# A gated embedding at the end of a mixture-of-experts phase: its projection computed ahead of it for all eight row tiles, and a wait moved in an attention loop

## What is computed

```python
# attention, per block of 128 query rows and per head (4 heads, values 128 wide)
prob = jax.nn.softmax(jnp.where(causal, sc, neg), axis=-1)
attn = prob[:, :, 0] - lam * prob[:, :, 1]
blocks.append(jnp.einsum('bhqk,bhkv->bhqv', attn.astype(v.dtype), v[:, :, :end]))

# after the mixture of experts: x is (1024, 1024), p is (1024, 256)
x = x + hierarchical_moe(rms_norm(x, norm_ffn[l]), ...)
ple_gate = jax.nn.sigmoid(rms_norm(x, norm_ple[l]) @ w_ple_gate[l])   # (1024, 1024)
x = x + ple_gate * (p[l] @ w_ple_proj[l])                             # (256, 1024)
```

## Time and profile before

| | us |
|---|---|
| median of 3 runs | 3212.57 (3206.74 to 3223.68) |
| the profiled execution | 3211.77 |
| its span, first to last instruction | 3209.9 |

### The profile page before, as it was taken

One profiled execution on the slowest core, in us unless ns is written; L12 is line 12 of the kernel. 1 busy time (PEld: TensorE's weight loads), 2 busy tenths in 40 slices (PEclk: granted clock), 3 DMA queues, 4 the chain that ended last, 5 costly groups with the idle time before them and its releaser, 6 DMA issues. The chain is left out here.

```text
span 3209.9 us, 52447 instructions
## 1 busy us (share of the span) xinstructions
PE 2899.2 (90%) x21080; PEld 2499.3 (78%) x21080; DVE 1898.4 (59%) x2347; ACT 1276.7 (40%) x1825; POOL 752.8 (23%) x474
## 2 busy tenths in 40 slices
PE   7999999888786897699999969799999998878898
PEld 7999997777454786588888848699999975756687
DVE  4365666775464543889898955420068668686411
ACT  3000015564554322588877743221111167443311
POOL 3222213332000000222221101168332252222300
PEclk9999999998687998799999979899999998896999
DMA  5457341001103732799999963534757662222411
GB/s 177 160 193 245 121 143 48 33 33 60 40 14 116 257 118 112 281 401 398 403 401 393 396 236 117 141 102 156 240 190 231 203 220 89 95 98 64 137 69 49
DMA packets 195579, 560.14 MB, mean 175 GB/s; under 512 B 26208, under 2 KB 99936, under 8 KB 169200
## 3 DMA queue, kind: packets, MB, share of 16 engines
q1 hardware_dynamic: 150000, 461.97, 40.0%
q10 hardware_dynamic: 34624, 64.17, 5.4%
q0 software_dynamic: 10752, 31.13, 3.1%
HBM read 440.10 MB, written 124.30 MB: 176 GB/s over the span
## 5 line engine op out<-in xcount | busy, mean ns | idle before, releaser
L437 PE MATMUL pin_psum<-pin_sb_w,pin_sb_hT 128*128 128x354 f32 (+1 forms) x5376 | 981.2, 344 | 15.2 <-DVE pin_sb_hT L373 6.0
L437 PEld LDWEIGHTS pin_psum<-pin_sb_w,pin_sb_hT 128*128 128x128 f32 x5376 | 938.0, 190 | 54.7 <-issue 8.1
L4510 DVE TENSOR_TENSOR moe_sb_wlo<-moe_sb_raw,moe_sb_whi 128x2048 fp32r<-128x2048 f32 x192 | 433.8, 2286 | 69.5 <-ACT moe_sb_whi L4279 69.5
L4279 ACT ACTIVATE moe_sb_whi<-moe_sb_raw 128x2048 fp32r<-128x2048 f32 x192 | 365.4, 1917 | 103.9 <-PE moe_psum L4649 77.6
L345 ACT ACTIVATE pin_sb_xt<-pin_psum,pin_sb_ss 128x353 f32<-128x353 f32 (+1 forms) x112 | 63.4, 587 | 508.8 <-PE pin_psum L437 433.3
L408 DVE TENSOR_SCALAR pin_sb_xt<-pin_psum,pin_sb_ss 128x353 f32<-128x353 f32 (+1 forms) x112 | 69.0, 625 | 294.3 <-PE pin_psum L437 294.1
L4649 PE MATMUL moe_psum<-moe_sb_whi,moe_sb_xhi 128*128 128x512 f32 x512 | 204.2, 399 | 8.4 <-DVE moe_sb_xlo L4514 8.4
L4649 PE MATMUL moe_psum<-moe_sb_whi,moe_sb_xlo 128*128 128x512 f32 x512 | 201.0, 393 | 0.0
L4649 PE MATMUL moe_psum<-moe_sb_wlo,moe_sb_xhi 128*128 128x512 f32 x512 | 200.5, 392 | 0.0
L294 POOL TENSOR_TENSOR pin_sb_w<-pin_sb_raw,pin_sb_w 128x2832 fp32r<-128x2832 f32 (+1 forms) x26 | 186.9, 7188 | 22.5 <-issue 19.8
L292 POOL CAST pin_sb_w<-pin_sb_raw 128x2832 fp32r<-128x2832 f32 (+1 forms) x26 | 74.4, 2863 | 486.1 <-PE pin_psum L437 462.7
(11 more groups left out here) (714 smaller groups left out, 5668.2 us busy)
## 6 DMA issues: line engine op xcount, KB each, us to landing
moe_sb_raw<-in_w_gate SPq DMA_DIRECT2D x64, 1024.0 KB
moe_sb_raw<-in_w_up SPq DMA_DIRECT2D x64, 1024.0 KB, 7.8
moe_sb_raw<-in_w_down SPq DMA_DIRECT2D x64, 1024.0 KB, 7.6
scratch_proj<-pin_sb_xt ACTq DMA_DIRECT2D x16, 1412.0 KB, 8.7
scratch_proj<-pin_sb_xt ACTq DMA_DIRECT2D x12, 1792.0 KB, 7.3
pin_sb_raw<-in_w_in SPq DMA_DIRECT2D x15, 1412.0 KB, 9.6
pin_sb_raw<-in_w_in SPq DMA_DIRECT2D x11, 1792.0 KB, 8.9
scratch_ybuf<-moe_sb_yb ACTq DMA_DIRECT2D x32, 512.0 KB, 8.3
```

Source lines behind the costliest of these rows:

```text
L437: mm = te.matmul(ps[:, t, 0:cols], hT[a_part][:, k, t * P:(t + 1) * P], wt[b][w_part][:, k, :], start=(k == 0 and n == 0), stop=(k == KD - ...
L4279: s.activation(whi[q][:, :, :], raw[q][:, :, :], ACT.Copy).then_inc(hi, 1)
L4510: tt(wlo[q][:, :, :], raw[q][:, :, :], whi[q][:, :, :].bitcast(F32), ALU.subtract).then_inc(lo, 1)
```

## The change

In **attention**, `output` no longer waits for both rounds of `flat_out` before its first instruction. The two transposes have no such wait, the first four matmuls wait for the first round alone, and the others for the second.

In **`moe_ple`**:

- p comes in one transfer of 1 MB (`pt`, all tiles) ahead of the weights, instead of 128 KB per tile beside `xt`.
- The weight tiles are loaded and split in another order: the two of the projection first.
- PE turns p of four tiles at a time (`turn_p`, eight transposes), once before the last `down` and once after it; ACT and DVE split each four (`round_p`, `rest_p`).
- PE computes all eight projections (`product_p`) right after the last `down`, into three pairs of banks in turn, in the order of tiles 1 to 7 and then 0. ACT copies the first six into SBUF (`keep_p`), four of them into the buffers `l_raw` once these are free; the last two stay in PSUM.
- `turn`, `copy` and `body` of the loop lose what they did with p: two transposes, one rounding, one subtraction, 12 matmuls per tile. `finish` reads the kept projection from SBUF (PSUM for tiles 7 and 0) and multiplies in place.
- One root of a dummy value, before the first `norm`, brings ACT's table for the root in ahead of time.

```diff
@@ class Attention, output
-                te.wait_ge(flat_out, rounds_to(i + 1))
                 te.wait_ge(kept, i + 1)
                 if t + 1 < NT:
                     for a in pair:
                         te.transpose(ps[:, 7, (2 + a) * P:(3 + a) * P], qk[t + 1][...], ident[:, :])
                 for k in range(t + 1):
+                    if k % 4 == 0:
+                        te.wait_ge(flat_out, rounds_to(i) + k // 4 + 1)
                     mm = te.matmul(ps[:, 7, 0:AV], aT[i % 2][:, k * P:(k + 1) * P], vv[k][...], start=(k == 0), stop=(k == t))
@@ moe_ple
+    W_ORDER = (KD, KD + 1, *range(KD))
+    P_ORDER, P_BANKS, KEPT = (*range(1, NT), 0), (2, 4, 6, 2, 4, 6, 2, 6), NT - 2
...
@@ sync
                 sp.dma_start(xt[b][:, :], x[t * P:(t + 1) * P, :]).then_inc(l_x_in[b], 16)
-                sp.dma_start(pt[b][:, :, :].rearrange("p a c -> p (a c)"), p[t * P:(t + 1) * P, :]).then_inc(l_x_in[b], 16)
...
+            sp.wait_ge(xt_ps, last_n + 1)
+            sp.dma_start(pt[:, :, :], p.rearrange("(t p) c -> p t c", p=P)).then_inc(p_in, 16)
             sp.wait_ge(lo, item(last_n, 1))
@@ scalar
-                s.activation(hThi[b][:, :, :], hT[:, :, :], ACT.Copy)
-                s.activation(pThi[b][:, :, :], blocks(ps, 2, 2), ACT.Copy).then_inc(rounded.sem, 1)
+                s.activation(hThi[b][:, :, :], hT[:, :, :], ACT.Copy).then_inc(rounded.sem, 1)
...
+            def round_p(i):
+                s.wait_ge(p_turned, i + 1)
+                s.activation(p_hi[i][:, :, :], blocks(ps, 0, 8), ACT.Copy).then_inc(p_high, 1)
+            def keep_p(j):
+                s.wait_ge(p_sums, j + 1)
+                if j >= 2:
+                    s.wait_ge(w_lo, KW)
+                s.activation(p_kept[j][:, :], banks(ps, P_BANKS[j]), ACT.Copy).then_inc(p_out, 1)
...
+            s.activation(ss[1][:, 2:3], ss[1][:, 2:3], ACT.Sqrt)
@@ vector
-                tt(pTlo[b][:, :, :], blocks(ps, 2, 2), pThi[b][:, :, :].bitcast(F32), ALU.subtract).then_inc(copied.sem, 1)
...
-                tt(m[:, :], l_sg[:, :], banks(ps, 6), ALU.mult)
+                tt(l_sg[:, :], l_sg[:, :], part, ALU.mult)
                 ve.drain()
-                tt(x_t[:, :], x_t[:, :], m[:, :], ALU.add).then_inc(added.sem, 1)
+                tt(x_t[:, :], x_t[:, :], l_sg[:, :], ALU.add).then_inc(added.sem, 1)
@@ tensor
+            def turn_p(i):
+                if i == 0:
+                    te.wait_ge(p_in, 16)
+                else:
+                    te.wait_ge(p_low, i)
+                for n in range(8):
+                    mm = te.transpose(block_of(ps, 0, n), pt[:, P_ORDER[4 * i + n // 2], ...], ident)
+                mm.then_inc(p_turned, 1)
+            def product_p(j):
+                i, at = j // 4, 2 * (j % 4)
+                if j % 4 == 0:
+                    te.wait_ge(p_low, i + 1)
+                if j == 0:
+                    te.wait_ge(w_lo, 2)
+                if j == 1:
+                    te.wait_ge(y_ev, last_n + 3)
+                if j >= 3:
+                    te.wait_ge(p_out, P_BANKS[:j][::-1].index(P_BANKS[j]) * -1 + j)
+                ...   # 12 matmuls into banks P_BANKS[j] and the next one
+            turn_p(0)
             down(last_n, tail=True)
+            turn_p(1)
+            for j in range(NT):
+                product_p(j)
@@ body(t)
-                te.wait_ge(added.sem, added.done(t - 1))
-                for half in range(2):
-                    for k in range(2):
-                        mm = product(6, proj_rows, b, KD, 2, half, k)
-                mm.then_inc(proj_sums.sem, 1)
```

More of the change, by code:

```diff
@@ L4124, in moe_ple @@
                       for i, n in enumerate(("hThi", "hTlo")))
-        xt = [put(f"xt{b}", [P, D], home["xb"] + D * b) for b in range(2)] + [put(f"xt{b}", [P, D], home["yb"] + D * (b - 2)) for b in (2, 3)]
-        pt = [put(f"pt{b}", [P, 2, P], home["xT"] + 2 * P * b) for b in range(AHEAD)]
-        pThi, pTlo = ([put(f"{n}{b}", [P, 2, P], home["xT"] + D + 2 * P * (2 * i + b), F32R) for b in range(2)]
-                      for i, n in enumerate(("pThi", "pTlo")))
+        xt = [put(f"xt{b}", [P, D], home["xT"] + D * b) for b in range(2)] + [put(f"xt{b}", [P, D], home["yb"] + D * (b - 2)) for b in (2, 3)]
+        pt = put("pt", [P, NT, 2 * P], home["xb"])
+        p_hi, p_lo = [put("p_hi0", [P, KD, P], home["a"], F32R), hThi[1]], [put("p_lo0", [P, KD, P], late, F32R), hTlo[1]]
+        p_kept = [put("p_kept0", [P, D], home["a"] + D), put("p_kept1", [P, D], late + 2 * D), *l_raw]
         l_sg = put("l_sg", [P, D], home["a"])
@@ L4708, in product @@
                 return mm
-            gate_rows, proj_rows = (hThi, hTlo), (pThi, pTlo)
+            gate_rows = (hThi, hTlo)
             def gate_half(t, half):
```

98 lines of the change are left out of this document (62 added, 36 removed).

## The result

| | kernel before | changed kernel |
|---|---|---|
| median | 3211.73 (3206.74 to 3223.68, 4 runs) | 3173.78 (3171.04 to 3175.19, 4 runs) |
| profiled execution, its span | 3211.77, 3209.9 | 3174.87, 3173.0 |

The ratio is 0.9874, 95% interval 0.9856 to 0.9893. The forecast was 3187, its range 3178 to 3201: the direction was right, the time 13 us too high and outside the range.

A forecast was written before the change was run, and what follows sets the result against it. The prediction saw PE's stops on a ring with ACT bounding wide attention, and PE, closely followed by a DVE-ACT ring, the embedding's loop. 8.4 + 3.1 + 0.6 + 10.1 + 2.2 = 24.4 us off 3211.77 gave 3187, range 3178 to 3201.

The forecast's parts named there:

- 8.7 + 0.7 - 1.0 = 8.4: Attention: us gained from PE's stops in wide steps, less what stays in tile 7; bounds 3 to 9.4.
- a swinging clock: Rival in the embedding's loop: PE's new pauses make its clock swing mildly, about 1.2 us a tile, 3194; chance 0.12.
- Cover of 0.75 against stops of 0.54: Attention: two transposes and four matmuls, 0.75 us, cover PE's wait for the second copy, 0.54 on average, 0.8 at most.
- The expected rest in tile 7: Attention: tile 7 lacks transposes, 0.5 us of cover against 0.7; some 0.25 may stay in each of four steps.
- Between experts and embedding: PE's added projections and ACT's copies fit the 24.80 us idle gap before the loop: cost 0, upper bound some 20 us.
- ACT ends near 1911: Between experts and embedding: ACT's copies and dummy root end near 1911, against idle until 1911.63; tight, but covered.
- First tile: Embedding's first tile: table load 1.1 us earlier, stretch from `turn(0)` 6.7 to 4.7; together -3.1, bounds -1.5 to -4.6.
- The loop: Embedding's loop, body(1) to the last sigmoid: six tiles from 89.3 to 79.2 us, -10.1, bounds -6 to -13.
- The ring: Embedding's loop: DVE and ACT, weigh to weigh, 14.03 falling to 13.1 us; x's load makes it 13.4 in four tiles.
- both slow-clock rivals: Embedding's loop: PE's clock swings mildly, 3194, chance 0.12; or the half behind each pause runs at 1.2 GHz, 3218, 0.04.
- The tail: Embedding's end: `finish` of the last tile no longer waits for the projection, -2.2 us.
- p's transfer: Ahead of the weights: p lands about 1882, in time for `down` at 1883.24, cost 0; a rival feared 38 us.

The follow-up runs named there:

- the repeat with 173.5 us: The changed kernel, unchanged, measured and profiled once more: 3177.26 us, 0.9874 of the kernel before; attention 173.5 us from first to last `keep`.
- the kernel best: Changed kernel with `finish` split into DVE's gaps, tile 0's gate in halves, dummy root earlier: 3167.18 us, 0.9863 of the kernel before; again 3167.95, 0.9846.

## Why the prediction was wrong

**Attention: the step that failed, by a mechanism left out.** The prediction's "8.7 + 0.7 - 1.0 = 8.4" with "Bounds: 3 to 9.4" priced a stop at its own length and nothing else. Attention alone gained 21.5 us. The stops proper are worth 9.4 of the wide steps' 20.5, so this part of the reading was sound, if a microsecond small. Left out was what they did to the clock, a term put at nothing without a reason. It was in the table of stages, 0.84 for the wide steps, and the prediction used a swinging clock as a rival only where the change adds pauses, not as a gain where it takes them away. Filling the stops without removing a wait gave 11.1 of the 20.5 us (6.4 to 6.7 of them in steps that repeat from profile to profile). The last 7 us of the first profile's 28.5 come and go between executions of the same kernel, as the repeat with 173.5 us shows. TensorE: Matmul & The Clock Gate, section "A second HAM failure mode: psum-queue depth-cycling", of the Trainium skill, which the prediction answered with "The trace has no such loop", says that short idle spells between groups can move the clock. The trace had such a loop, in rows 1 and 2 that the prediction used itself: attention, where stops of 0.4 to 0.9 us went with 0.51 of the clock in step 18, and not in the loop, where 0.80 and 0.32 us per tile of 13.4 did nothing. The length of one pause doesn't decide it: the 1.91 us of the earlier trace rows, on which the prediction leaned, left the clock at 1.00, and 1.94 us in the kernel best were followed by 0.50.

**Counting a stop.** Cover of 0.75 against stops of 0.54 was sound in its result, though the stops are longer than printed (0.63 for 0.47). A step at full clock gained 0.6 to 0.9 us (steps 19 to 28). The expected rest in tile 7 didn't stay: no wait is left before its matmuls.

**Between experts and embedding: right, to about 1.4 us.** PE's cost was at most 0.2: the last matmul of the projections started at 1887.59 and turn(0) at 1887.82, and `h` was ready at 1887.61 (DVE's 0.75 from 1886.86). "ACT ends near 1911" had 0.6 us to spare; in the profile ACT is free only 1.3 us after weigh(0) has ended (1885.03 against 1883.72), since its last copy waits for PE, and PE's projections for copies that wait for the last weight.

**First tile: right where the gather lands late.** turn(0) spans 1.03 and is followed by body(0) after 4.70, both as forecast. But weigh(0) to turn(0) grew to 6.75 from 6.44 by that overhang, the dummy root's table load in it. With the embedding changed alone, and a gather that landed 1.3 us later after its issue, it is 5.34: the 1.1 us less that was forecast. The drain of about 1.38 us that ScalarE: Activation LUTs, section "What ACT_TABLE_LOAD costs", of the Trainium skill, states beside the load again doesn't show: the load runs from 1883.62 for 1.28 us and the root follows at 1884.92.

**The loop: right to 0.9 us, by a wrong ring.** The ring is 13.42 with or without a transfer of x, not 13.1: `pThi` and `pTlo` took 0.27 and 0.34 from start to start, where the prediction took their durations and hand-overs, 0.37 and 0.58. The transfer arrives just then, so the 13.4 of the prediction came out, but by luck: the ring alone gives it, and the profile names `xt` as releaser at 1951.14 and not at 1937.72, both at 13.42. In two other profiles x does add to the ring, 0.3 and 0.4 us in one tile and 0.1 and 0.2 in another. PE's clock stayed at 1.00 from 1915 to the loop's end and both slow-clock rivals fell; the pause was 0.80 at the turn and 0.32 at the next half, 1.1 in all.

**The tail and p's transfer: right.** 2.1 us for 2.2; 7.4 us to landing.

**The range** left no room above attention's bound of 9.4, and so ended at 3178.
